# Rows, probabilities, keys and values turned by four 64x64 products instead of one 128x128 transposition, in a hybrid encoder step on one core

## The chip, the cores and the metric

One NeuronCore of a Trainium2 chip runs the whole program in one launch. The metric is the device time of that core in microseconds (us), the median of the runs. All data is float32; the large products are made from two rounded parts (below).

## The reference

One inference step of a one-layer encoder, for 512 prompt tokens and 8 samples of 16 tokens (640 tokens, width 1024). What bears on the change:

```python
h = rmsnorm(x, norm_mix_g);  parts = split_cols(h @ w_in)        # gated delta rule, short convolution, stick-breaking attention
rhs = concatenate([v * beta[..., None], k * (beta * exp(gc))[..., None]])   # delta rule: scaled values and keys
S_new = S * exp(g_last) + einsum('tk,tv->kv', k * exp(g_last - gc)[..., None], v_new)
x = x + concatenate([y_a, y_b, y_c]) @ w_mix_out
h = rmsnorm(x, norm_mem_g); qm = rmsnorm(h @ w_mq, mq_norm_g)    # memory attention, 256 memory tokens, 4 heads
x = x + (softmax(qm @ mem_k.T / sqrt(128)) @ mem_v) @ w_mo
h = rmsnorm(x, norm_ffn_g)
x = x + (silu(dwconv3(h @ w_gate)) * (h @ w_up)) @ w_down
```

## The kernel before

The tokens are five tiles of 128 (four of the prompt, n = 0 to 3, and one of all samples, n = 4, PT in the code). Each engine has an instruction list of its own, written out by hand: TensorE from line 430, ScalarE, GpSimd, and VectorE from line 2136. Engines meet by semaphores: a product bank (PSUM, eight banks of 128x512) is taken with `take`, declared full with `done`, waited for with `filled`, released by its reader and waited for again with `evacuated`. The order on an engine is the program's; nothing is planned at run time.

A large product `a @ w` is three products of rounded parts (hi x hi, hi x lo, lo x hi) in a fast float32 form; ScalarE cuts the hi parts (line 1599 for weights), VectorE the lo parts (line 2150). These products fill most of TensorE's time. Products between plain float32 tiles (in the delta rule and the attentions) each show as two records in the profile.

The places where something is turned from token rows to columns, or back, are:

- **Norm rows**, `turn_rows` (line 571), for norm2 before memory attention and norm3 before the feed-forward part, five tiles each. Eight 128x128 transpositions (line 577) put the 1024 columns of a tile into two banks, four in each. The first bank is declared full after the first four. ScalarE copies each bank to `hhi` (line 1612), VectorE subtracts to get `hlo` and releases it (line 2160). The turns stand between large products: norm2's two first together (lines 1009 and 1010), norm3's between the products with `w_mo` and the first gate products (lines 1171 to 1185).
- **Memory probabilities**, `mem_probs` (line 1088), the same with line 1094, five tiles; ScalarE copies to `probT` (line 2009).
- **Values and keys of the delta rule**, `turn_vk` (line 847), five tiles: four transpositions of the values into bank `Vt`, four of the keys into `Kt` (line 853). VectorE's `vk_part` (line 2420) makes three scaled copies of 128x512: values by beta (2425), keys by bege (2428, after which `kd_ready` lets TensorE's `w_part`, line 885, go on) and keys by kdec (2430).

The order around the delta rule's chunks is: `w_part(4)`, `w_part(0)`, `turn_vk(1)`, then for each chunk i the product `vn` (line 960), `w_part(i + 1)` (line 891), `dS` (971), `o` (977), `turn_vk(i + 2)`.

Products of 64x64 on quarters of the array are in the kernel already: the triangular inverse (`level_products`, line 821) runs them on all four, lines 836 and 842, eight of each line in a step; steps 64-row transpositions (868) and products (875, 881) on one quarter.

```python
                for h in range(HEADS):
                    if y is not None:
                        for g in range(2):
                            last_y = T.matmul(y[half64(1 - g), h, :], lmb[n % LM_RING][half64(g), h, :],
                                              Xb[i][half64(g), h, :], start=True, stop=True)
                    if dx is not None:
                        for g in range(2):
                            last_dx = T.matmul(dx[half64(g), h, :], Xb[i2][half64(g), h, :], XTb[i2][half64(g), h, :],
                                               start=True, stop=True)
```

Of the kernel before, what the change touches and what calls it, by code (L numbers as in the profile page):

```python
# [5 lines left out]
F32 = mybir.dt.float32  # L6
# [5 lines left out]
P = 128  # L12
# [55 lines left out]
def hybrid_step(nc, A, O):  # L68
    ctx = ExitStack()
    with ctx:  # L70
# [208 lines left out]
        def quad(b):  # L279
            return bank[b][:, :].rearrange("p (a b) -> p a b", a=4)  # L280

# [148 lines left out]
        def _(pe):  # L430
# [139 lines left out]

            def turn_rows(kind, n, src, ready):

                pe.wait_ge(s["xn_ready"], ready)
                for g in range(2):
                    b = take((kind, n, g))
                    for j in range(4):
                        ins = T.transpose(bank[b][:, j * P:(j + 1) * P], src[:, (4 * g + j) * P:(4 * g + j + 1) * P],
                                          ident[:, :])
                    done(ins, (kind, n, g))
# [267 lines left out]
            def turn_vk(i):  # L847

                tt = slice(i * P, (i + 1) * P)
                for name, f0 in (("Vt", 8), ("Kt", 4)):  # L850
                    b = take((name, i))
                    for h in range(HEADS):
                        ins = T.transpose(bank[b][:, h * P:(h + 1) * P], qkvz[:, f0 + h, tt], ident[:, :])
                    done(ins, (name, i))
# [54 lines left out]
            def sample_new():  # L909
                pe.wait_ge(s["st_loaded"], 16 * DEC_BATCH)  # L910
                evacuated(pe, ("wT", PT))
                evacuated(pe, ("Vt", PT))
# [26 lines left out]
            def sample_states(h):  # L939
                evacuated(pe, ("Kt", PT))  # L940
# [10 lines left out]
            for i in range(PT):  # L951
                tt = slice(i * P, (i + 1) * P)
                evacuated(pe, ("Vt", i))
# [13 lines left out]
                evacuated(pe, ("Kt", i))  # L967
# [70 lines left out]
            for h, tiles in ((0, (0, 1, 2)), (1, (3, PT))):  # L1038
                for n in tiles:
                    for g in range(2):  # L1040
                        evacuated(pe, ("norm2", n, g))
                across_half(("mq", 0), B_MQ[0], h)
# [45 lines left out]
            def mem_probs(i):  # L1088
                pe.wait_ge(s["prob_ready"], i + 1)
                for g in range(2):  # L1090
                    b = take(("pT", i, g))
# [4 lines left out]
                    done(ins, ("pT", i, g))  # L1096
# [483 lines left out]
        def _(act_e):  # L1580
# [28 lines left out]
            def hi_part(kind, n, dst):  # L1609
                for g in range(2):  # L1610
                    b = filled(e, (kind, n, g))
                    V(dst[:, 4 * g:4 * g + 4], quad(b), ACT.Copy).then_inc(s["h_hi_ready"], 1)
# [303 lines left out]
            for i in range(PT):  # L1916
# [10 lines left out]
                elif i == 2:  # L1927
                    o_part(PT)
                    filled(e, ("Kt", PT - 1))
                    y_hi(0)  # L1930
# [73 lines left out]
            def prob_turned(i):  # L2004
                if i >= 2:
                    filled(e, ("om", i - 2))
                for g in range(2):
                    b = filled(e, ("pT", i, g))
                    V(probT[i % 2][:, 2 * g:2 * g + 2, :, :].rearrange("p h n t -> p (h n t)"), bank[b][:, :], ACT.Copy)\
# [126 lines left out]
        def _(dve):  # L2136
# [18 lines left out]
            def lo_part(kind, n, hi, lo):  # L2155
                for g in range(2):
# [3 lines left out]
                    V.tensor_tensor(lo[:, 4 * g:4 * g + 4], quad(b), hi[:, 4 * g:4 * g + 4].bitcast(F32), ALU.subtract)\  # L2160
# [732 lines left out]
```

## Time and profile before

| | us |
|---|---|
| median of three runs | 947.84 (947.35 to 947.84) |
| the profiled execution | 947.93 |
| its span, first to last instruction | 946.2 |
| TensorE busy | 934.1 (99%) |
| VectorE busy | 648.3 (69%) |
| ScalarE busy | 451.9 (48%) |
| GpSimd busy | 170.1 (18%) |
| transfers | 103.69 MB, 16 engines busy 32% of the span |

The span is shorter than the time of its execution by 1.7 us, which lie before the first and after the last instruction. An engine's busy time is the union of its records. TensorE's records overlap, since one product drains while the next fills, so a record's own duration (some 270 ns for a 128x128 transposition) is not what it costs; the distance from one start to the next is.

### The profile page before, as it was taken

What the parts mean: (1) busy time and instruction counts of PE and PEld (TensorE: products, weight loads), DVE (VectorE), ACT (ScalarE), POOL (GpSimd) and SP (SyncE); (2) the same over time, 40 slices, a digit from 0 to 9 for tenths busy, and PEclk for the clock granted to TensorE, in tenths of its full rate; (3) what the DMA queues carried; (4) which work ended last, traced back from release to release, by engine and by line L of the source; (5) the groups of instructions that cost most, each with busy time, mean ns of one, the idle gap of its engine ahead of it and who ended that gap; (6) DMA issues with size and microseconds to landing.
All of it is one profiled execution on the core that took longest, in us unless ns stands there. A gap on an engine that the chain in (4) does not pass through costs nothing.

```text
span 946.2 us, 16664 instructions
## 1 busy us (share of the span) xinstructions
PE 934.1 (99%) x6807; PEld 847.1 (90%) x6807; DVE 648.3 (69%) x1083; ACT 451.9 (48%) x836; POOL 170.1 (18%) x198
## 2 busy tenths in 40 slices
PE   8999999999999999999999999999999999999998
PEld 7899888998889877899889999999999999888886
DVE  7627888777775556551666999999999999435321
ACT  6634444648565344464655445444444446333310
POOL 0071101103654331000002042222222220000000
PEclk9999999999999999999999999999999999999999
DMA  8624152121104084143903322222222224312221
GB/s 302 225 87 145 56 169 90 48 94 46 45 5 134 2 278 166 61 150 150 317 35 116 132 90 90 89 90 90 76 74 77 87 89 147 152 59 97 76 91 55
DMA packets 73819, 103.69 MB, mean 110 GB/s; under 512 B 2576, under 2 KB 53904, under 8 KB 73360
## 3 DMA queue, kind: packets, MB, share of 16 engines
q1 hardware_dynamic: 73744, 102.63, 32.0%
q8 instruction: 54, 0.88, 0.4%
q14 instruction: 21, 0.17, 0.1%
HBM read 92.27 MB, written 10.35 MB: 108 GB/s over the span
## 4 chain that ended last, share of the span: by engine, by line
PE 90%; DVE 4%; ACT 2%; issue 1%; POOL 1%; DMA 1%; SPq 0%; ACTq 0%; DVEq 0%; POOLq 0%
PE bank L1202 8%; PE bank L1204 8%; PE bank L1203 8%; PE bank L533 7%; PE bank L535 7%; PE bank L534 7%; PE bank L495 6%; PE bank L497 5%; PE bank L496 5%; PE bank L463 3%; PE bank L559 2%; PE bank L561 2%; PE bank L560 2%; PE bank L482 1%; PE bank L481 1%; PE bank L483 1%
## 5 line engine op out<-in xcount | busy, mean ns | idle before, releaser
L2150 DVE TENSOR_TENSOR wlo<-wraw,whi 128x2048 fp32r<-128x2048 f32 (+1 forms) x56 | 126.1, 2253 | 103.1 <-ACT whi L1599 93.8
L1599 ACT ACTIVATE whi<-wraw 128x2048 fp32r<-128x2048 f32 (+1 forms) x58 | 109.3, 1885 | 102.7 <-PE bank L535 72.9
L495 PE MATMUL bank<-hhi,whi 128*128 128x320 f32 x352 | 116.4, 331 | 0.6 <-issue 0.6
L497 PE MATMUL bank<-hhi,wlo 128*128 128x320 f32 x352 | 108.7, 309 | 0.0
L496 PE MATMUL bank<-hlo,whi 128*128 128x320 f32 x352 | 108.7, 309 | 0.0
L495 PEld LDWEIGHTS bank<-hhi,whi 128*128 128x128 f32 x352 | 66.2, 188 | 5.0 <-issue 3.6
L496 PEld LDWEIGHTS bank<-hlo,whi 128*128 128x128 f32 x352 | 66.2, 188 | 3.0 <-issue 2.4
L497 PEld LDWEIGHTS bank<-hhi,wlo 128*128 128x128 f32 x352 | 66.1, 188 | 0.0
L533 PE MATMUL bank<-whi,hhi 128*128 128x512 f32 x150 | 58.4, 389 | 0.0
L534 PE MATMUL bank<-wlo,hhi 128*128 128x512 f32 x150 | 58.4, 389 | 0.0
L535 PE MATMUL bank<-whi,hlo 128*128 128x512 f32 x150 | 58.3, 389 | 0.0
L1567 POOL TENSOR_TENSOR traw_up<-wraw 128x512 f32<-128x512 f32 x10 | 14.3, 1428 | 196.2 <-PE bank L1204 170.7
L1202 PE MATMUL bank<-hhi,whi 128*128 128x320 f32 x152 | 47.1, 310 | 0.0
L1204 PE MATMUL bank<-hhi,wlo 128*128 128x320 f32 x152 | 47.0, 309 | 0.0
L1202 PE MATMUL bank<-shi,whi 128*128 128x320 f32 x152 | 47.0, 309 | 0.0
L1203 PE MATMUL bank<-slo,whi 128*128 128x320 f32 x152 | 47.0, 309 | 0.0
L1204 PE MATMUL bank<-shi,wlo 128*128 128x320 f32 x152 | 47.0, 309 | 0.0
L1203 PE MATMUL bank<-hlo,whi 128*128 128x320 f32 x152 | 47.0, 309 | 0.0
L2524 DVE TENSOR_TENSOR xres<-xres,bank 128x512 f32<-128x512 f32 x30 | 20.1, 685 | 26.4 <-PE bank L535 18.8
L2248 DVE SCALAR_TENSOR_TENSOR act<-cb,flanes,act 128x512 f32<-128x512 f32 x44 | 33.0, 749 | 0.9
L534 PEld LDWEIGHTS bank<-wlo,hhi 128*128 128x128 f32 x150 | 28.2, 188 | 5.9
L533 PEld LDWEIGHTS bank<-whi,hhi 128*128 128x128 f32 x150 | 28.2, 188 | 5.9
(489 smaller groups left out, 2701.9 us busy)
## 6 DMA issues: line engine op xcount, KB each, us to landing
wraw<-in_w_in SPq DMA_DIRECT2D x13, 1024.0 KB, 5.3
wraw<-in_w_gate SPq DMA_DIRECT2D x11, 1024.0 KB, 5.1
wraw<-in_w_up SPq DMA_DIRECT2D x11, 1024.0 KB, 5.1
wraw<-in_w_down SPq DMA_DIRECT2D x10, 1024.0 KB, 5.0
kTs<-in_cache_sb_k SPq DMA_DIRECT2D x8, 512.0 KB, 4.4
vraw<-in_cache_sb_v SPq DMA_DIRECT2D x8, 512.0 KB, 5.0
wraw<-in_w_mix_out SPq DMA_DIRECT2D x4, 1024.0 KB, 6.1
kmT<-in_cache_mem_k SPq DMA_DIRECT2D x8, 512.0 KB, 6.0
```

Source lines behind the costliest of these rows:

```text
L495: T.matmul(o, wh[:, k, cs], hhi[:, k, hs], start=(k == 0), stop=False)
L496: T.matmul(o, wh[:, k, cs], hlo[:, k, hs], start=False, stop=False)
L497: ins = T.matmul(o, wl[:, k, cs], hhi[:, k, hs], start=False, stop=(k == KD - 1))
L533: T.matmul(o, hi[:, t * P:(t + 1) * P], wh[:, kk, :], start=(k == 0), stop=False)
L534: T.matmul(o, hi[:, t * P:(t + 1) * P], wl[:, kk, :], start=False, stop=False)
L535: ins = T.matmul(o, lo[:, t * P:(t + 1) * P], wh[:, kk, :], start=False, stop=(k == nk - 1))
L1202: T.matmul(o, w[0][:, k, :], a[0][:, k, :], start=(k == 0), stop=False)
L1203: T.matmul(o, w[0][:, k, :], a[1][:, k, :], start=False, stop=False)
L1204: ins = T.matmul(o, w[1][:, k, :], a[0][:, k, :], start=False, stop=(k == half_block - 1))
L1599: V(wv(whi, i), wv(wraw, i), ACT.Copy).then_inc(s["w_hi_ready"], 1)
L2150: V.tensor_tensor(wv(wlo, i), wv(wraw, i), wv(whi, i).bitcast(F32), ALU.subtract)\
L2248: V.scalar_tensor_tensor(out=out[:, 0:SEQ], in0=a, scalar=w[:, k:k + 1], in1=out[:, 0:SEQ], op0=ALU.mult, op1=ALU.add)
```

## The change

A new helper turns eight 128x128 pieces, each by four ordinary products with the identity: source rows g (a half of 64), source columns c, to output partitions c, 64 columns wide. Row half g of all eight pieces goes to bank g, so that a bank now holds eight pieces of 64 columns where it held four of 128. Both banks are taken ahead, and both are declared full at the end. Norm rows, memory probabilities of the four prompt tiles, and values with keys use it; the sample tile's probabilities stay as they were. Readers take the new layout with the same number of instructions, except `vk_part`, where each of the three scalings becomes two of half the size, and both banks are released by the last pair.

```diff
+        def eighths(b):
+            return bank[b][:, :].rearrange("p (a b) -> p a b", a=8)
...
+            def turn_quarters(outs, srcs):
+
+                for j, src in enumerate(srcs):
+                    last = []
+                    for g in range(2):
+                        for c in range(2):
+                            ins = T.matmul(bank[use[outs[g]][0]][half64(c), BLOCK * j:BLOCK * j + BLOCK],
+                                           src[half64(g), half64(c)], ident[half64(g), half64(g)], start=True, stop=True)
+                        last.append(ins)
+                for ins, key in zip(last, outs):
+                    done(ins, key)
+
             def turn_rows(kind, n, src, ready):
 
                 pe.wait_ge(s["xn_ready"], ready)
-                for g in range(2):
-                    b = take((kind, n, g))
-                    for j in range(4):
-                        ins = T.transpose(bank[b][:, j * P:(j + 1) * P], src[:, (4 * g + j) * P:(4 * g + j + 1) * P],
-                                          ident[:, :])
-                    done(ins, (kind, n, g))
+                outs = [(kind, n, g) for g in range(2)]
+                for key in outs:
+                    take(key)
+                turn_quarters(outs, [src[:, k * P:(k + 1) * P] for k in range(KD)])
...
             def turn_vk(i):
 
                 tt = slice(i * P, (i + 1) * P)
-                for name, f0 in (("Vt", 8), ("Kt", 4)):
-                    b = take((name, i))
-                    for h in range(HEADS):
-                        ins = T.transpose(bank[b][:, h * P:(h + 1) * P], qkvz[:, f0 + h, tt], ident[:, :])
-                    done(ins, (name, i))
+                outs = [("VKt", i, g) for g in range(2)]
+                for key in outs:
+                    take(key)
+                turn_quarters(outs, [qkvz[:, f0 + h, tt] for f0 in (8, 4) for h in range(HEADS)])
...
-            for h, tiles in ((0, (0, 1, 2)), (1, (3, PT))):
-                for n in tiles:
-                    for g in range(2):
-                        evacuated(pe, ("norm2", n, g))
+            turned = [(n, g) for n in range(NT) for g in range(2)]
+            for h in range(2):
+                for n, g in turned[NT * h:NT * h + NT]:
+                    evacuated(pe, ("norm2", n, g))
                 across_half(("mq", 0), B_MQ[0], h)
...
             def hi_part(kind, n, dst):
                 for g in range(2):
                     b = filled(e, (kind, n, g))
-                    V(dst[:, 4 * g:4 * g + 4], quad(b), ACT.Copy).then_inc(s["h_hi_ready"], 1)
+                    V(dst[:, :, half64(g)], eighths(b), ACT.Copy).then_inc(s["h_hi_ready"], 1)
...
             def vk_part(i):
-                b = filled(dve, ("Vt", i))
                 slots = (smp_v, smp_kb, smp_kd) if i == PT else (scr[i % 2], scr[2 + i % 2], scr[4 + i % 2])
+                bs = [filled(dve, ("VKt", i, g)) for g in range(2)]
                 if 2 <= i < PT:
                     filled(dve, ("dS", i - 2))
-                V.tensor_tensor(slots[0][:, :, :], quad(b), spread(beta[:, i, :], 2, [P, HEADS, P]), ALU.mult)\
-                    .then_inc(bank_free[b], 1)
-                b = filled(dve, ("Kt", i))
-                V.tensor_tensor(slots[1][:, :, :], quad(b), spread(bege[:, i, :], 2, [P, HEADS, P]), ALU.mult)\
-                    .then_inc(s["kd_ready"], 1)
-                V.tensor_tensor(slots[2][:, :, :], quad(b), spread(kdec[:, i, :], 2, [P, HEADS, P]), ALU.mult)\
-                    .then_inc(bank_free[b], 1)
+                for out, heads, scale in ((slots[0], slice(0, 4), beta), (slots[1], slice(4, 8), bege), (slots[2], slice(4, 8), kdec)):
+                    for g, b in enumerate(bs):
+                        ins = V.tensor_tensor(out[:, :, half64(g)], eighths(b)[:, heads, :],
+                                              spread(scale[:, i, :], 2, [P, HEADS, BLOCK]), ALU.mult)
+                        if out is slots[2]:
+                            ins.then_inc(bank_free[b], 1)
+                    if out is slots[1]:
+                        ins.then_inc(s["kd_ready"], 1)
```

What moves in the instruction lists. TensorE at `turn_vk(1)`, before the change (lines 891, 853 and 960 are `w_part`, the turn and `vn`; the number at a bank or buffer tells which one it is):

```order
L891 MATMUL bank5<-XT0_93,scr2_55 128x128 x3
L853 MATMUL bank0<-ident_259,qkvz_191 128x128 [waits bank_free0]
L853 MATMUL bank0<-ident_259,qkvz_191 128x128 x3
L853 MATMUL bank1<-ident_259,qkvz_191 128x128 [waits bank_free1]
L853 MATMUL bank1<-ident_259,qkvz_191 128x128 x3
L960 MATMUL bank2<-scr0_53,XT0_93 128x128 [waits bank_free2,bank_free5,bank_free7]
L960 MATMUL bank2<-scr0_53,XT0_93 128x128 x3
L891 MATMUL bank3<-XT1_94,scr3_56 128x128 [waits bank_free3,kd_ready,bank_free2]
```

The same place in the changed kernel, where lines 907 and 976 are `w_part` and `vn`:

```order
L907 MATMUL bank5<-XT0_93,scr2_55 128x128 x3
L580 MATMUL bank0<-ident_259,qkvz_191 64x64 [waits bank_free1,bank_free0]
L580 MATMUL bank0<-ident_259,qkvz_191 64x64
L580 MATMUL bank1<-ident_259,qkvz_191 64x64 x2
L580 MATMUL bank0<-ident_259,qkvz_191 64x64 x2
...
L976 MATMUL bank2<-scr0_53,XT0_93 128x128 [waits bank_free5,bank_free2,bank_free7]
L976 MATMUL bank2<-scr0_53,XT0_93 128x128 x3
L907 MATMUL bank3<-XT1_94,scr3_56 128x128 [waits bank_free3,kd_ready,bank_free2]
```

Eight instructions became thirty-two, two to a bank in turn, and the neighbours stand where they stood. VectorE's scalings for the same turn, before:

```order
L2462 TENSOR_TENSOR sqG1_160<-yb_195 128x640
L2425 TENSOR_TENSOR scr1_54<-bank0,beta_297 128x512
L2428 TENSOR_TENSOR scr3_56<-bank1,bege_306 128x512
L2430 TENSOR_TENSOR scr5_58<-bank1,kdec_305 128x512
L2492 COPY stP0_131<-bank4 128x512
```

and in the changed kernel:

```order
L2485 TENSOR_TENSOR sqG1_160<-yb_195 128x640
L2449 TENSOR_TENSOR scr1_54<-bank0,beta_297 128x4x64
L2449 TENSOR_TENSOR scr1_54<-bank1,beta_297 128x4x64
L2449 TENSOR_TENSOR scr3_56<-bank0,bege_306 128x4x64
L2449 TENSOR_TENSOR scr3_56<-bank1,bege_306 128x4x64
L2449 TENSOR_TENSOR scr5_58<-bank0,kdec_305 128x4x64
L2449 TENSOR_TENSOR scr5_58<-bank1,kdec_305 128x4x64
L2515 COPY stP0_131<-bank4 128x512
```

The first of them needs both banks now, and `kd_ready` comes behind four instructions instead of two.

## Rows read from the trace of the kernel before

**Rows 1.** The page: the chain that ended last, by engine.
```profile
PE 90%; DVE 4%; ACT 2%; issue 1%; POOL 1%; DMA 1%; SPq 0%; ACTq 0%; DVEq 0%; POOLq 0%
```

**Rows 2.** Span and mean granted TensorE clock.
```profile
core 0: 946.2 us, clock 1.000
```

**Rows 3.** Groups by line and form, TensorE: count | busy us, mean ns | idle before.
```profile
L836 PE MATMUL bank<-Xb,lmb 64*64 64x64 f32 x368 | 14.0, 222 | 0.4 <-issue 0.4
L577 PE MATMUL bank<-ident,xn 128*128 128x128 f32 x80 | 10.3, 273 | 0.0
```

**Rows 4.** Timeline, TensorE, turn of norm3's last tile: start us, us, records.
```profile
521.22 0.31 PE L483 MATMUL bank<-hhi,wlo 128*128 128x320 f32 x1
521.36 1.04 PE L577 MATMUL bank<-ident,xn 128*128 128x128 f32 x8
522.15 0.39 PE L481 MATMUL bank<-hhi,whi 128*128 128x320 f32 x1
522.38 0.31 PE L482 MATMUL bank<-hlo,whi 128*128 128x320 f32 x1
```

**Rows 5.** Timeline, TensorE, 32 quarter products of the triangular inverse.
```profile
261.50 0.31 PE L496 MATMUL bank<-hlo,whi 128*128 128x320 f32 x1
261.64 0.31 PE L497 MATMUL bank<-hhi,wlo 128*128 128x320 f32 x1
261.88 0.27 PE L836 MATMUL bank<-Xb,lmb 64*64 64x64 f32 x2
...
262.05 0.23 PE L836 MATMUL bank<-Xb,lmb 64*64 64x64 f32 x2
...
262.75 0.23 PE L836 MATMUL bank<-Xb,lmb 64*64 64x64 f32 x2
...
262.97 0.42 PE L495 MATMUL bank<-hhi,whi 128*128 128x320 f32 x1
263.23 0.31 PE L496 MATMUL bank<-hlo,whi 128*128 128x320 f32 x1
```

**Rows 6.** Timeline, TensorE, turns of the delta rule among plain float32 products.
```profile
287.98 1.08 PE L868 MATMUL bank<-ident,XT 64*64 64x64 f32 x16
288.99 1.09 PE L853 MATMUL bank<-ident,qkvz 128*128 128x128 f32 x8
290.01 1.90 PE L875 MATMUL bank<-Xb,LT 64*64 64x64 f32 x29
...
296.23 1.04 PE L853 MATMUL bank<-ident,qkvz 128*128 128x128 f32 x8
...
298.26 1.13 PE L891 MATMUL bank<-XT,scr 128*128 128x128 f32 x8
...
300.37 1.06 PE L977 MATMUL bank<-qkD,scr 128*128 128x128 f32 x8
301.26 1.04 PE L853 MATMUL bank<-ident,qkvz 128*128 128x128 f32 x8
302.13 1.24 PE L898 MATMUL bank<-sqG,same 128*128 128x320 f32 x4
```

**Rows 7.** Timeline, VectorE, scalings of one turn, and two smaller operations from a bank.
```profile
283.56 0.85 DVE L2448 TENSOR_TENSOR XT<-XTb,bank 64x256 f32<-64x256 f32 x2 [0.38 <-PE bank L842]
...
296.87 0.69 DVE L2425 TENSOR_TENSOR scr<-bank,beta 128x512 f32<-128x512 f32 x1 [1.02 <-PE bank L853]
297.48 0.68 DVE L2428 TENSOR_TENSOR scr<-bank,bege 128x512 f32<-128x512 f32 x1
```

**Rows 8.** Timeline, TensorE, three waits after turns: idle us and releaser in brackets.
```profile
401.14 0.47 PE L1022 MATMUL bank<-whi,mhi 128*128 128x512 f32 x1 [0.89 <-DVE wlo L2150]
...
475.74 0.47 PE L559 MATMUL bank<-whi,omhi 128*128 128x512 f32 x1 [0.32 <-DVE wlo L2150]
...
481.95 0.47 PE L559 MATMUL bank<-whi,omhi 128*128 128x512 f32 x1 [0.58 <-DVE omlo L2598]
```

**Rows 9.** The same timeline, the last turn of probabilities before that third wait.
```profile
480.33 1.04 PE L1094 MATMUL bank<-ident,probs 128*128 128x128 f32 x8
```

More of the change, by code:

```diff
@@ L849, in turn_vk, with values_keys_done @@
                 tt = slice(i * P, (i + 1) * P)
-                for name, f0 in (("Vt", 8), ("Kt", 4)):
-                    b = take((name, i))
-                    for h in range(HEADS):
-                        ins = T.transpose(bank[b][:, h * P:(h + 1) * P], qkvz[:, f0 + h, tt], ident[:, :])
-                    done(ins, (name, i))
+                outs = [("VKt", i, g) for g in range(2)]
+                for key in outs:
+                    take(key)
+                turn_quarters(outs, [qkvz[:, f0 + h, tt] for f0 in (8, 4) for h in range(HEADS)])
+            def values_keys_done(i):
+                for g in range(2):
+                    evacuated(pe, ("VKt", i, g))
             for n in range(len(LM_ORDER) + LAG):
@@ L911, in sample_new @@
                 evacuated(pe, ("wT", PT))
-                evacuated(pe, ("Vt", PT))
+                values_keys_done(PT)
                 b = take(("vn", PT), long=True)
@@ L939, in sample_states @@
             def sample_states(h):
-                evacuated(pe, ("Kt", PT))
+                values_keys_done(PT)
                 pe.wait_ge(s["vm_ready"], h + 1)
@@ L952, in _ @@
                 tt = slice(i * P, (i + 1) * P)
-                evacuated(pe, ("Vt", i))
+                values_keys_done(i)
                 evacuated(pe, ("wT", i))
@@ L966, in _ @@
                 evacuated(pe, ("vn", i))
-                evacuated(pe, ("Kt", i))
+                values_keys_done(i)
                 vn = scr[8 + i % 2]
@@ L1089, in mem_probs @@
                 pe.wait_ge(s["prob_ready"], i + 1)
+                outs = [("pT", i, g) for g in range(2)]
+                if i < PT:
+                    for key in outs:
+                        take(key)
+                    turn_quarters(outs, [probs[i % 2][:, h, nb * P:(nb + 1) * P] for h in range(HEADS) for nb in range(2)])
+                    return
                 for g in range(2):
-                    b = take(("pT", i, g))
+                    b = take(outs[g])
                     for j in range(4):
@@ L1095, in mem_probs @@
                                           ident[:, :])
-                    done(ins, ("pT", i, g))
+                    done(ins, outs[g])
             def mem_values(i):
@@ L1928, in _ @@
                     o_part(PT)
-                    filled(e, ("Kt", PT - 1))
+                    filled(e, ("VKt", PT - 1, 1))
                     y_hi(0)
@@ L2008, in prob_turned @@
                     b = filled(e, ("pT", i, g))
-                    V(probT[i % 2][:, 2 * g:2 * g + 2, :, :].rearrange("p h n t -> p (h n t)"), bank[b][:, :], ACT.Copy)\
+                    V(probT[i % 2][:, :, :, half64(g)].rearrange("p h n t -> p (h n) t"), eighths(b), ACT.Copy)\
                         .then_inc(bank_free[b], 1)
@@ L2159, in lo_part @@
                     b, _ = use[(kind, n, g)]
-                    V.tensor_tensor(lo[:, 4 * g:4 * g + 4], quad(b), hi[:, 4 * g:4 * g + 4].bitcast(F32), ALU.subtract)\
+                    V.tensor_tensor(lo[:, :, half64(g)], eighths(b), hi[:, :, half64(g)].bitcast(F32), ALU.subtract)\
                         .then_inc(bank_free[b], 1)
```

## The prediction

> **What bounds the kernel now.** I read the page first. TensorE is busy for 934.1 of 946.2 us, and 90% of the chain that ended last is its own work [rows 1]. So the kernel is a queue of products, and a change pays only as far as it makes TensorE's list shorter, or removes one of the few waits in it. The granted clock is 1.000 over the span, the higher level of 2.4 GHz [rows 2]; there is no slow stretch to win back. The second thing to read is what a turn costs as a distance between starts, since durations overlap (a mean of 273 ns for a transposition whose 80 records make 10.3 us busy) [rows 3]. The third is where TensorE waits near a turn, for there a longer or shorter turn is free [rows 8]. The changed stretches lie between 283 and 530 us; the 416 us of feed-forward work behind them only shift.
>
> **What eight transpositions cost.** Between large products, norm3's last turn starts at 521.36 and the gate product behind it at 522.15 [rows 4]. From the start of the last large product ahead (521.22) to the second one behind (522.38) it is 1.16 us, of which two starts of such products, some 0.145 us each (261.50 to 261.64 [rows 5], 521.22 to 521.36), would have been there anyway: 0.87 us, or 0.109 each. Among plain float32 products it is the same 0.87 us, 301.26 to 302.13 [rows 6].
>
> **What thirty-two quarter products cost.** The triangular inverse holds the very burst: 16 calls of line 836 and 16 of line 842 on all four quarters, between the same large products. From 261.64 to 263.23 it is 1.59 us [rows 5], less the same 0.29: 1.29 us. Two things are in it. First the stream: twelve steps from 262.05 to 262.75, so 58 ns for a group of four records, one on each quarter. A product leaves two records (368 for 184 calls) [rows 3], a transposition one (80 for 80). So a piece needs two groups, 117 ns, where one transposition took 109: eight pieces are 0.93 us against 0.87, **0.06 us more**. The four quarters do run at once, but the plain product goes twice through them. Second the change of width: 1.29 less 0.93 is **0.36 us** for going in and out. It is seen as 0.24 us ahead of the first quarter product where 0.145 is the step, and 0.26 from 262.97 to 263.23 behind them [rows 5]. A turn among large products thus costs 0.42 us more.
>
> Among plain float32 products the two changes cost less. Eight transpositions between quarter work take 1.02 us (288.99 to 290.01) against 0.87, and the sixteen one-quarter transpositions ahead, 56 ns apart, 1.01 us against 0.90 [rows 6]. Half a change each way, with the slower first step behind: I take 0.29 us for both, so 0.35 us more for such a turn. Bounds for a turn: 0.06 if the width changes cost nothing, 0.42 if they always cost what they do at large products.
>
> **The sum, place by place** (TensorE, in order).
>
> - *Norm2.* Tiles 0 and 1 form one burst: 2 x 0.06 + 0.36 = 0.48. Tile 2: 0.42. Tile 3 is followed by an idle 0.89 us until 401.14, for a weight cut on VectorE [rows 8] that comes from ScalarE's cut, which waited for an earlier product: 0.42 hides there, 0. Tile 4, between memory-key products: 0.42. Together 1.3.
> - *Norm3.* Tile 0 already follows a change of width (32-wide products) and has transpositions behind: one way only, 0.2. Tiles 1 to 4: 4 x 0.42 = 1.7. Together 1.9.
> - *Probabilities.* Four turns, 0.35 + 0.2 (products of 32 columns follow, a change that is there already) + 0.42 + 0.42 = 1.4 of TensorE's time. But VectorE and ScalarE pace this stretch: TensorE waits 0.32 and 0.58 us idle at 475.74 and 481.95 [rows 8]. By the distance of starts the second is 0.75 (480.33 plus 0.87 is 481.20 [rows 9]), so an idle time leaves out some 0.17, and the two are 1.2 in all. What comes out is 0.2.
> - *Values and keys.* Turn 4 follows quarter work, so loses one change it paid (0.15) and gains the dear one behind (0.22) with 0.06: 0.1. Turn 0 stands between quarter products: it loses both changes, 0.06 - 0.29 = -0.2. Turns 2 and 3 are among plain products: 0.35 each. Turn 1 is longer by a wait: `w_part(1)` at 298.26 starts 0.1 us after VectorE's second scaling ends (297.48 + 0.68) [rows 6, 7]. That scaling chain started 0.64 us into the turn (296.87), with the first bank. Now both banks come at the end, about 1.25 us into it (0.09 + 0.05 + 0.93 and the drain), 297.5. Then four half scalings stand before `kd_ready` instead of two. A half costs between 0.30 us (half of the 0.61 between two starts) and 0.43 (two 64x256 operations from a bank in 0.85) [rows 7]; I take 0.40, nearer to the row of that size. 297.5 + 1.6 + 0.1 = 299.2, 0.95 later; the product behind waits a little for a copy of ScalarE's that is there by then, so I take 0.8. Bounds 0.4 and 1.0. Together 1.4. The other scalings have idle VectorE around them (1.02 us before this one [rows 7]); without it they would cost 0.6 a turn.
> - *Readers.* ScalarE and VectorE keep their counts at norm rows and probabilities, but start some 0.6 us later, since the first bank no longer comes early. The waits of TensorE behind a turn are those of rows 8, and none names these readers, since other products stand between; so 0. The finer wait for norm2 (2.5 tiles instead of 3 for the first query half) frees nothing: other products cover it. No transfer moves.
>
> Sum: 1.3 + 1.9 + 0.2 + 1.4 = **4.8 us more**. The profiled execution took 947.93, 0.09 above the median of the runs shown, so 952.7, or **952.6** as a median. A measurement of this kernel tells 0.2% (1.9 us) from no change: below 945.9 is faster, above 949.7 slower.
>
> **The rivals.**
>
> - *One group does a piece* (the other side). A product with the identity, whose records may pair differently from those of the inverse, goes through the four quarters once, 58 ns for a piece. A tile then costs 0.47 us. With the changes of width kept, a single turn at large products is 0.83 against 0.87 (six of them -0.2), the double saves 0.4, norm3's first turn 0.3 and values and keys 1.0, and the sum is -1.9: 946.0, no change. If these changes also fade, it saves 0.40 on each of the some 14 tiles that nothing else paces, 942. It decides from a piece below 64 ns on, where the 0.36 are earned back. For it: nothing but that the moving side is always the same. Against: two records for every plain product in the trace. Chance 0.11, of which 0.08 for the faster form. The Trainium skill, page "TensorEngine Tiling (Array Packing)", section "Theoretical Speedup", gives a factor of up to 2 for each side of 64 or less, so 4 for these; as an estimate, eight pieces in 0.22 us, which lands in the same rival.
> - *Cover is larger than I see.* The readers' and the later stages' waits take most of it, or the changes of width are half of what the inverse shows, since its bursts start with waits for banks: 0.15 to 0.2 a turn, some 1.5 us in all. 949.3, no change. For it: the first step after each wait is slow anyway. Against: the exit, 0.26 for 0.147, has no wait. Chance 0.1.
> - *A new wait.* Late banks push ScalarE and VectorE where they pace TensorE (481.95) and around each chunk; a further 0.6 us at five places, 955.6. For it: the second bank's copy ends 0.6 later everywhere. Against: idle readers before most turns. Chance 0.1.
> - *Quarters in one row half do not overlap.* The inverse never issues two neighbours of one row half; here all do. Pairs in turn would double the stream: 0.93 more for 19 tiles, 968. Against: in the inverse all four still run within one group. Chance 0.04. The Trainium skill, page "TensorE: Matmul & The Clock Gate", section "Terms", has transpose mode four times faster than a plain product for float32, which speaks against this change and lands here too: a piece would take four groups, not two, an estimate. The rows have two records per product; the sum goes by them.
> - That the change does not do what it says is excluded: the lists show the 32 products and six scalings.
>
> **How the numbers follow.** The forecast has 0.65, its own range 951 to 954.5 (0.06 to 0.42 a turn would be wider, but the burst of the same size fixes it). Faster: 0.08, the first rival's faster form. Same: 0.03 of its weaker form and 0.1 of the second, 0.13. Slower: 0.65 + 0.1 + 0.04 = 0.79. The range, 949.0 to 956.0, takes in the new wait and the upper half of the second rival, and leaves out 946.0, 942, 968 and the lower half, 0.2 in all.
>
> **What would show it.** Right: the product line of the new helper with 1216 records (19 tiles x 64), groups of four 58 ns apart; 1.29 us between large products; 64x64 at 0.24 ahead and 0.25 behind; `w_part(1)` about 0.95 us later against its turn's start; the idle of 0.89 before the first memory-key product nearly halved; the wait before 481.95 gone or small; a half scaling near 0.40 us. Wrong: 608 records, or groups of 29 ns; a turn under 0.9 us; idle growing behind turns; or a gain in the feed-forward part, which the change does not touch.

## The result and the profile after

The changed kernel takes **955.37 us** (median of four runs, 955.09 to 956.57), the kernel before 947.84 (947.35 to 948.23) beside it: a ratio of 1.0081, interval 1.0066 to 1.0096. That is 7.5 us more; the forecast was 4.8 more, 952.6, with a range to 956.0, and the forecast's own part of it ended at 954.5. Of all executions of all variants one stands apart (row halves, 1295 us at a mean granted clock of 0.663), and the ratios leave it out. The profiled execution took 955.46 with a span of 953.7. The page of the changed kernel, its parts 1, 3 (queues) and 4 (chain):

```profile
PE 941.1 (99%) x7871; PEld 851.5 (89%) x7871; DVE 649.5 (68%) x1098; ACT 451.9 (47%) x836; POOL 170.1 (18%) x198
...
q8 instruction: 62, 1.02, 0.5%
...
PE 92%; DVE 3%; ACT 2%; POOL 1%; issue 1%; DMA 1%; SPq 0%; ACTq 0%; POOLq 0%; DVEq 0%
```

TensorE is still the chain [rows 1]; it has 7.0 us more of busy time (934.1 before) and 1064 records more (6807 before). The second row is the one I had not thought about: the page calls queue 8 "instruction", and it moved 62 packets of 16 KB where the kernel before moved 54:

```profile
q8 instruction: 54, 0.88, 0.4%
```

These packets are TensorE's own list. Its weight loads, products and semaphore operations together are 16051 records, 62.7 times 256; before they were 13910, 54.3 times 256. In all fourteen traces the packets are this quotient to within one. The span's mean granted clock is 1.000, as in [rows 2].

The new helper's line, and one turn between large products (start, us, records), which answers to [rows 4]:

```profile
L580 PE MATMUL bank<-ident,xn x640: 218/218/267, 389.5 to 529.5; 64*64 64x64 f32 x160
L580 PE MATMUL bank<-ident,qkvz x320: 218/218/268, 283.7 to 316.0; 64*64 64x64 f32 x160
L580 PE MATMUL bank<-ident,probs x256: 218/218/267, 465.9 to 487.4; 64*64 64x64 f32 x128
```

```profile
528.32 0.31 PE L486 MATMUL bank<-hhi,wlo 128*128 128x320 f32 x1
528.56 1.16 PE L580 MATMUL bank<-ident,xn 64*64 64x64 f32 x64
529.65 0.42 PE L484 MATMUL bank<-hhi,whi 128*128 128x320 f32 x1
529.90 0.31 PE L485 MATMUL bank<-hlo,whi 128*128 128x320 f32 x1
```

640 + 320 + 256 are the 1216 records forecast, two for each product. The turn goes in after 0.24, streams for 0.94 (16 groups 58 ns apart), and out in 0.15 + 0.25: 528.32 to 529.90 is 1.58, less two steps 1.29. That is the figure taken from the inverse.

The turn that costs most is the delta rule's second, with the wait behind it. It answers to [rows 6], where `w_part(1)` starts 2.03 us after its turn (296.23 to 298.26). TensorE's products, its weight loads and VectorE's scalings:

```profile
297.35 1.16 PE L580 MATMUL bank<-ident,qkvz 64*64 64x64 f32 x64
298.44 1.16 PE L976 MATMUL bank<-scr,XT 128*128 128x128 f32 x8
301.53 1.05 PE L907 MATMUL bank<-XT,scr 128*128 128x128 f32 x8 [1.93 <-issue]
```

```profile
298.88 0.53 PEld L976 LDWEIGHTS bank<-scr,XT 128*128 128x128 f32 x4
300.16 0.19 PEld L907 LDWEIGHTS bank<-XT,scr 128*128 128x128 f32 x1 [0.76 <-issue]
301.53 0.86 PEld L907 LDWEIGHTS bank<-XT,scr 128*128 128x128 f32 x7 [1.19 <-issue]
```

```profile
298.67 0.76 DVE L2449 TENSOR_TENSOR scr<-bank,beta 128x256 f32<-128x256 f32 x2 [1.96 <-PE bank L580]
299.34 0.75 DVE L2449 TENSOR_TENSOR scr<-bank,bege 128x256 f32<-128x256 f32 x2
300.01 0.75 DVE L2449 TENSOR_TENSOR scr<-bank,kdec 128x256 f32<-128x256 f32 x2
```

Here it is 4.18 us after its turn. The semaphore wait ended at 300.16, when the first weights of `w_part(1)` were loaded, just behind the keys' second half scaling (299.34 + 0.75). That is the forecast wait. But the second load comes only at 301.53. Nothing in the profile holds it ("issue"), and its data is there: the first load had the same wait in front.

### The profile page after: what moved, and what is told of

It reads as the page before. It is cut to its first block, busy times and chain, and to the rows that moved or that the text cites. A ratio compares the mean times of both kernels' runs of the same rounds, so it can differ in the third digit from the quotient of the medians.

```text
span 953.7 us, 18825 instructions
## 1 busy us (share of the span) xinstructions
PE 941.1 (99%) x7871; PEld 851.5 (89%) x7871; DVE 649.5 (68%) x1098; ACT 451.9 (47%) x836; POOL 170.1 (18%) x198
## 4 chain that ended last, share of the span: by engine, by line
PE 92%; DVE 3%; ACT 2%; POOL 1%; issue 1%; DMA 1%; SPq 0%; ACTq 0%; POOLq 0%; DVEq 0%
PE bank L1224 8%; PE bank L1226 8%; PE bank L1225 8%; PE bank L536 7%; PE bank L538 7%; PE bank L537 7%; PE bank L498 6%; PE bank L500 5%; PE bank L499 5%; PE bank L466 3%; PE bank L580 2%; PE bank L562 2%; PE bank L564 2%; PE bank L563 2%; PE bank L484 2%; PE bank L485 1%
```

## The experiments

Two theories of the missing 2.7 us. **W**, the waits of late banks and half scalings are longer than I had them, at `w_part(1)` above all. **F**, instruction fetch: the list is brought in pieces of 256 records, and a list with 128 records a turn where 16 stood runs dry. F came from counting TensorE's records in order of start. Every gap of TensorE that nothing else explains lies ahead of a record that is 193 to 195 modulo 256 (short: record 195; a count by start is off by one or two), 1.2 to 1.6 us behind the landing of a packet of queue 8. The reverse holds too: in none of the fourteen traces does TensorE pass this place sooner than 1.2 us behind the landing of the packet that belongs to it (record 256k + 449 and packet k, both counted from 0). The first four experiments set F against W, the later ones settle one point each.

**Norm rows alone** (values, keys and probabilities as before; the edit for values and keys, against the changed kernel):

```diff
-                outs = [("VKt", i, g) for g in range(2)]
-                for key in outs:
-                    take(key)
-                turn_quarters(outs, [qkvz[:, f0 + h, tt] for f0 in (8, 4) for h in range(HEADS)])
+                for name, f0 in (("Vt", 8), ("Kt", 4)):
+                    b = take((name, i))
+                    for h in range(HEADS):
+                        ins = T.transpose(bank[b][:, h * P:(h + 1) * P], qkvz[:, f0 + h, tt], ident[:, :])
+                    done(ins, (name, i))
...
```

> The norm rows alone are turned by quarter products; probabilities, values and keys as before. Both theories price these ten tiles alike, from the trace of the changed kernel: 0.54 + 0.43 + 0 + 0.39 us in norm2 and 0.17 + 0.45 + 0.40 + 0.49 + 0.39 in norm3, so 3.3 us over the kernel before, 951.1, ratio 1.0034. If the stretches cost less alone (late banks in one place pushing another), under 2.5 us.

950.91 (five runs), ratio 1.0033 (1.0020 to 1.0046): 3.0 us more, my sum for the ten turns being 3.2. This part of the forecast stands.

**Values and keys alone** (norm rows and probabilities as before):

> Values and keys alone are turned by quarter products, with the halved scalings. Theory W (width changes, a longer stream and scalings that start late, as forecast): 1.4 us over before, 949.2. Theory F (besides, TensorE's sequencer waits for its next piece of instruction list, 16 KB for 256 instructions, since a turn now holds 128 instructions instead of 16): the instruction list up to w_part(1) is that of the changed kernel, so the gap in issue of some 1.4 us between its first and second weight load returns, and the whole is 2.5 to 3.3 us over before, 950.3 to 951.1.

951.59, ratio 1.0034 (1.0021 to 1.0047): 3.7 more, against 1.4 in my sum, and above F's 950.3 to 951.1 too. TensorE's timeline at `w_part(1)`, here line 909:

```profile
297.24 1.16 PE L580 MATMUL bank<-ident,qkvz 64*64 64x64 f32 x64
298.33 1.16 PE L978 MATMUL bank<-scr,XT 128*128 128x128 f32 x8
301.97 1.05 PE L909 MATMUL bank<-XT,scr 128*128 128x128 f32 x8 [2.48 <-issue]
```

The wait is longer than in the change (2.48 for 1.93) with the same scalings. W has no reason for that. The packet of queue 8 starts at 299.43 here and at 298.93 in the change.

**The list shifted.** 32 idle quarter products near the program's start, 128 records, and nothing else:

```diff
                 T.matmul(bank[7][:, 0:P], ones[:, :], ones[:, :], start=True, stop=True)
+            for n in range(8):
+                for g in range(2):
+                    for c in range(2):
+                        T.matmul(bank[7 - g][half64(c), 0:BLOCK], ones[half64(g), half64(c)], ones[half64(g), 0:BLOCK],
+                                 start=True, stop=True)
```

> The changed kernel with 32 idle quarter products on a constant added to TensorE's list at its very start, where TensorE waits for data anyway: 128 instructions, half of a 16 KB piece. Theory F: the gap in w_part(1) moves elsewhere or changes its size by 0.5 us or more, other gaps in issue between 255 and 300 us move too, and total time changes by up to 1.5 us either way. Theory W: the gap stays where it is with its 1.4 us within 0.2, since the semaphores are the same; total within 0.5 us of the changed kernel.

952.11, ratio 1.0042 (1.0028 to 1.0056): with more work, 3.3 us faster than the change. W allowed 0.5; F has the direction open and had named up to 1.5, so its size was missed as well. `w_part(1)`, here line 912, has no gap behind its first load:

```profile
296.52 1.16 PE L580 MATMUL bank<-ident,qkvz 64*64 64x64 f32 x64
297.61 1.16 PE L981 MATMUL bank<-scr,XT 128*128 128x128 f32 x8
299.37 1.13 PE L912 MATMUL bank<-XT,scr 128*128 128x128 f32 x8 [0.59 <-issue]
```

It starts 2.85 us after its turn, 0.82 later than in the kernel before. So W is real there and as large as the forecast had it (0.8), and the other 1.3 of 4.18 were the list.

**Keys scaled first**, so that `kd_ready` needs two half scalings fewer:

```diff
-                for out, heads, scale in ((slots[0], slice(0, 4), beta), (slots[1], slice(4, 8), bege), (slots[2], slice(4, 8), kdec)):
+                for out, heads, scale in ((slots[1], slice(4, 8), bege), (slots[0], slice(0, 4), beta), (slots[2], slice(4, 8), kdec)):
```

> The changed kernel with VectorE's two scalings of the keys by bege ahead of those of the values, so that kd_ready comes 0.66 us earlier. Theory W (w_part(1) waits for the scaling): w_part(1) starts 0.66 us earlier and the time falls by 0.5 to 0.7 us. Theory F (the instructions arrive later than the scaling): its first weight load starts 0.66 us earlier, the second not, and the time stays within 0.2 us.

955.24, ratio 1.0075 (1.0060 to 1.0090): no gain measured. In its profiled execution `w_part(1)` does start sooner, 2.48 us after its turn, but TensorE ran at the lower clock level in the stretch before (granted clock 0.50 from 294.8 to 296.7), which cost 1.5 us there. The packet landed at 298.96, 1.9 us before TensorE reached its records, so the list held nothing up at this place. All four runs have a mean clock of 0.998 or 0.999, against two of four in the change. The run tells little of W's size.

**One weight load held back** behind `w_part(1)`:

```diff
                 D(stS[:, bt, :, :], A["state_gdn"][bt].rearrange("h k v -> k h v")).then_inc(s["st_loaded"], 16)
+            filled(sp, ("wT", 1))
             load_w(B_OUT[1][0])
```

> The changed kernel, where SyncE holds back one load, the 1 MB of w_mix_out behind the eight state loads, until the product w_part(1) is done. TensorE's list is the same instruction for instruction. Fetch theory: the piece of TensorE's list that w_part(1) needs waits behind data on the DMA engines (there the fetch began 6.4 us after the last gap, elsewhere 1.3 to 1.9); with the states' 2 MB done by about 295 it begins near 296 instead of 298.93, the gap of 1.37 us ahead of w_part(1)'s second weight load goes, and the time falls by about 1.4 us, to 954.0. Rival (the gap is TensorE's own, from the place in its list or from the late scalings): the gap stays at 1.3 to 1.4 us, the fetch may come earlier, and the time is that of the changed kernel, 955.4. Second rival (the fetch begins at a fixed distance ahead of need and not behind data): fetch and gap stay as they are.

954.20, ratio 1.0066 (1.0054 to 1.0079): 1.2 less than the change, as F had it (1.4), though the two intervals overlap. Among runs with a mean clock of 1.000 it is about 2 less (953.0 and 953.5 here, 955.1 and 955.5 in the change). In the trace the packet starts at 297.08 and not 298.93, and `w_part(1)`'s second load follows its first without a gap. This execution had the lower clock level too (0.50 at 296.7 to 298.4), so the place can't be compared in time.

**Row halves.** The same pieces turned by two transpositions on half the rows:

```diff
                     for g in range(2):
-                        for c in range(2):
-                            ins = T.matmul(bank[use[outs[g]][0]][half64(c), BLOCK * j:BLOCK * j + BLOCK],
-                                           src[half64(g), half64(c)], ident[half64(g), half64(g)], start=True, stop=True)
+                        ins = T.transpose(bank[use[outs[g]][0]][:, BLOCK * j:BLOCK * j + BLOCK],
+                                          src[half64(g), :], ident[half64(g), half64(g)])
```

> The changed kernel, where each piece is turned by two transpositions on the two row halves of the array (64 rows in, 128x64 out) instead of four quarter products: 16 instructions a tile of one record each instead of 32 of two. All else (banks, eighths, half scalings) as in the change. If the two halves run at once, as the four quarters did, a step of 64 columns is 56 ns for a pair and a tile streams in 0.45 us instead of 0.93, so with the 0.36 of going in and out a turn is 0.81 at large products (0.87 in the kernel before). That gives against the changed kernel 0.48 a tile, some 16 tiles unpaced, 7.5 us, and with the lists' pieces elsewhere (1 us either way) 947 to 949: the loss gone, and what is left is the late banks. If the halves do not overlap, a tile takes 0.90 and the time is 953 to 955.

947.73 (median of eleven runs), ratio 0.9997 (0.9987 to 1.0006): all the loss is gone. The turn that answers to [rows 4]:

```profile
521.36 0.31 PE L486 MATMUL bank<-hhi,wlo 128*128 128x320 f32 x1
521.60 0.72 PE L579 MATMUL bank<-ident,xn 64*128 64x64 f32 x16
522.25 0.42 PE L484 MATMUL bank<-hhi,whi 128*128 128x320 f32 x1
522.50 0.31 PE L485 MATMUL bank<-hlo,whi 128*128 128x320 f32 x1
```

A pair takes 62 to 65 ns and a tile streams in 0.49 to 0.52 us: both halves run at once, and each transposition leaves one record, 16 for a tile where the quarter products leave 64. With the same change of width, 521.36 to 522.50 is 1.14, less two steps 0.85; the whole transpositions took 0.87. The stream halves and the change of width takes it back.

**The kernel before with the shifted list:**

> The kernel before, with the same 32 idle quarter products near the start that took 3.2 us off the changed kernel (64 instructions more in TensorE's list, nothing else). The kernel before shows three gaps of TensorE of its own between 264 and 277 us (0.43, 0.66, 0.43), each at a record that is 195 modulo 256, 1.3 to 1.6 us behind the landing of a piece of the list. Fetch theory: the three gaps move to other places; there they may be covered or not, so the time changes by up to 1.4 us either way, with every new gap again at 195 modulo 256, and 947 to 948.5 is likeliest. Rival (gaps belong to these products, not to the place in the list): they stay at the same products and the time is unchanged at 947.9 (plus 0 to 0.5 for the added work).

947.23 (eleven runs), ratio 0.9994 (0.9985 to 1.0002). The three gaps of 0.43 to 0.66 us are gone and two of 0.36 and 0.30 are there, at 269.30 and 273.69, again at record 195. What it saves, 0.7, can't be told from nothing. (The idle products are 128 records, not the 64 I gave there.)

**Row half by row half**, the order of the 32 products changed so that only two quarters can work at once:

```diff
-                for j, src in enumerate(srcs):
-                    last = []
-                    for g in range(2):
+                for g in range(2):
+                    for j, src in enumerate(srcs):
                         for c in range(2):
...
-                for ins, key in zip(last, outs):
-                    done(ins, key)
+                    done(ins, outs[g])
```

> The changed kernel with the same 32 quarter products of a turn in another order: first the 16 of the upper rows (two quarters, side by side in columns), then the 16 of the lower rows, and the first bank reported full halfway. It measures whether all four quarters work at once. If they do in the change, this order halves it: a group of two quarters takes 58 ns as a group of four did, a tile streams in 1.87 instead of 0.93 us, and 0.93 for 16 unpaced tiles make 970, less some 0.3 a turn where readers waited for the first bank. If the order of issue does not matter (the engine reorders, or the rate is one of issue, 14.5 ns a record), the time is 955 or less.

966.32, ratio 1.0196 (1.0182 to 1.0210). A turn, here between 512-wide products:

```profile
524.10 1.91 PE L579 MATMUL bank<-ident,xn 64*64 64x64 f32 x64
525.94 0.50 PE L562 MATMUL bank<-whi,omhi 128*128 128x512 f32 x1
```

1.84 us from the turn's start to the next product, where four quarters take 1.09. So in the change all four do work at once, and the rival of quarters that do not overlap is out. (The time expected was 970 less some 0.3 a turn.)

**Norm rows and probabilities by quarters**, values and keys as before:

> The changed kernel with norm rows and probabilities by quarter products, but values and keys as in the kernel before. The part with norm rows alone took 950.9; this adds the probabilities. The trace of the changed kernel has 0.57 us between the first of their turns and the last, 0.4 of it a gap at a place in the instruction list, which is elsewhere here. Forecast 951.2; by my sum 951.1; if VectorE's and ScalarE's later banks cost what the third rival of the prediction said (0.6 a chunk), 952.5 and more.

951.28, ratio 1.0039 (1.0026 to 1.0053). The probabilities cost 0.4 over norm rows alone, near the 0.2 of the sum.

**The list shifted by half as much** (`range(4)` for `range(8)`, 64 records):

> The changed kernel with half as many idle quarter products near the start, 16, so that every later place of TensorE's list moves by 64 records and not by 128. (The 32 of the earlier run were 128 records, loads and products counted: 16179 against 16051.) Fetch theory: the gaps go where a record is 195 modulo 256 now, the one of w_part(1) into the middle of the values' and keys' second turn (297.8), where everything behind it (the banks, the scalings, w_part(1)) is late too. If the fetch there again comes 6 us after the last one's gap, the time is 956 to 958, above the changed kernel with its smaller list; if it comes after 1.6 to 2.2 us as in the run shifted by 128, no gap is left and the time is 952 to 953. In neither case is there a gap of over 0.5 us at w_part(1)'s second load. Rival (the gap belongs to w_part(1), whatever its place in the list): 1.4 us there again and 955.4.

955.06, ratio 1.0078 (1.0066 to 1.0091): neither number of F's, and close to its rival's 955.4. But the trace is against the rival: `w_part(1)` starts 2.85 us after its turn (296.70 to 299.55), without a gap. The time is lost in a place that no expectation had named, between memory scores of the samples:

```profile
470.63 2.55 PE L1149 MATMUL bank<-kmT,qz 128*32 128x256 f32 x43
474.75 0.83 PE L1149 MATMUL bank<-kmT,qz 128*32 128x256 f32 x9 [1.58 <-issue]
```

The last weight load ahead of the gap starts 2.17 us earlier, and the gap ends at record 9410, which is 194 modulo 256. The kernel shifted by 128 has 0.40 there. F's rule for where a gap can be holds; how long the gap is depends on when the piece is fetched. The windows of queue 8 show that the packet starts after 472, 4.15 us after the record 195 of the piece before (467.88), with the DMA engines full. The queues in two windows, and the busy times of one (its last two columns are the DMA engines' share and GB/s):

```profile
q1 hardware_dynamic: 718, 1.38, 100.7%
```

```profile
q1 hardware_dynamic: 225, 0.43, 92.2%
q8 instruction: 1, 0.02, 6.0%
```

```profile
464.00:472.00 8.00, 8.00 (x193) 6.71 (x196) 5.28 (x15) 4.62 (x13) 0.31 (x1) 1.00 0.99 344
```

The first row is the whole of 467.9 to 472, without a packet of queue 8, the next two are 472 to 473.3.

The same trace shows a second wait, which is W's. Behind turn 0 the products of line 902 wait for a bank that VectorE's last scalings release:

```profile
289.88 2.03 PE L896 MATMUL bank<-Xb,LT 64*64 64x64 f32 x32
292.11 2.04 PE L902 MATMUL bank<-XT,Xb 64*64 64x64 f32 x32 [0.21 <-DVE scr L2454]
```

```profile
291.70 0.27 PE L881 MATMUL bank<-XT,Xb 64*64 64x64 f32 x1
```

Here they start 2.23 us after line 896; in the kernel before (second fence, its line 881) they start 1.69 us after line 875 at 290.01 [rows 6]. The run shifted by 128 has 2.23 as well and the change 2.24, so this 0.5 us is there wherever the list's pieces fall.

**Quiet load queues** there, with the same list:

```diff
                 load_mem_k(bt)
+            filled(sp, ("ms", PT, 1))
             for bt in range(3, 7):
                 load_mem_v(bt)
             for t in range(2):
                 evacuated(sp, ("mv", 0, t))
             D(O["p_mem_v"].rearrange("(t p) c -> p t c", p=P), memv[:, :, :]).then_inc(s["out_mv"], 16)
             load_w(B_GU[0][0])
-            filled(sp, ("ms", PT, 1))
```

> The kernel of e11_shifted_by_64, where SyncE holds back four loads of memory values, the output of memory values and the load of w_gate (3.5 MB in all, which run from 463 to 475) until the samples' memory scores are done at some 475.5. TensorE's list is the same instruction for instruction. It settles what delays a piece of the list. In e11_shifted_by_64 the record 9155 (195 modulo 256) starts at 467.88, the next piece is fetched only 4.15 us later, at 472.03, and TensorE stands 2.17 us ahead of record 9410 until 474.75. If a fetch waits behind the data of the load queue (DMA engines 0.97 to 1.00 busy there), it now begins within 1.1 to 2.1 us of 467.9, as in the stretch 260 to 285 without traffic, lands before 471, the gap of 2.17 goes and the time falls by about 2 us, to 953.1 (less if the late loads are waited for). If it always begins some 4 us behind in this part of the list, whatever the queues carry, gap and time stay, 955.1.

953.14, ratio 1.0053 (1.0040 to 1.0067): 1.9 us less than the same list with busy queues, the number expected. Queue 8 from 467.9 to 469.8, TensorE from 464 to 473.3, and its timeline:

```profile
q8 instruction: 1, 0.02, 3.2%
```

```profile
464.00:472.00 8.00, 8.00 (x187) 1.00 0.28 102
472.00:473.30 1.30, 1.30 (x26) 1.00 0.00 0
```

```profile
469.69 3.42 PE L1149 MATMUL bank<-kmT,qz 128*32 128x256 f32 x60
473.04 2.05 PE L1134 MATMUL bank<-probT,memv 128*128 128x128 f32 x16
```

The packet starts 1.05 us behind record 195 (467.37), lands before 470, and the gap is gone. Against the kernel before beside each run (947.69 and 948.20) the saving is 2.4. F is shown, and at this place also that the piece of TensorE's list came late because of the data of the loads.

**A version that beats both:** row halves for norm rows and probabilities, whole transpositions for values and keys, and the idle products.

> The attempt at a version that beats both. Norm rows and probabilities turned by two transpositions on the row halves, as in e6_row_halves; values and keys, their scalings and their two banks as in the kernel before; and the 32 idle quarter products near the start. From the rows of e6_row_halves beside those of the kernel before, a turn between large products is 0.03 us shorter than eight whole transpositions (1.30 against 1.33, and 1.14 against 1.17), the double one of norm2 0.41 shorter (1.81 against 2.22), norm3's first 0.1: some 0.8 us in all. The idle products gave the kernel before 0.7. Together 1.5: 946.4, a ratio of 0.9984. Rival: the readers, which start later because both banks fill at the end, take it back at the probabilities, and only the 0.7 of the idle products stays: 947.2.

946.61 (eleven runs), ratio 0.9990 (0.9981 to 0.9998): faster than the kernel before by 1.1 us, of 1.5 expected. Only the double turn gains much: from the large product ahead to the second behind it (384.48 to 386.29) it is 1.81 us.

```profile
384.48 0.39 PE L564 MATMUL bank<-whi,mxlo 128*128 128x512 f32 x1
384.80 1.22 PE L579 MATMUL bank<-ident,xn 64*128 64x64 f32 x32
385.95 0.50 PE L562 MATMUL bank<-whi,mxhi 128*128 128x512 f32 x1
386.29 0.40 PE L563 MATMUL bank<-wlo,mxhi 128*128 128x512 f32 x1
```

The kernel before takes 2.22 for the same. The gain is small, close to what this measurement tells from nothing, and 0.7 of it is what the idle products alone did for the kernel before.

## Why the prediction was right, and where it was short

The time came 2.7 us above the sum, outside the forecast's own 951 to 954.5. It fell inside the range only because the range had room for the rival of a new wait at 955.6: the direction is the forecast's merit, that 955.4 lies in the range is luck.

**Direction, stream and change of width: right.** Two records a product, 58 ns a group, 0.36 us in and out at large products, 1.29 for a turn: all as read from the inverse's burst. Compared place by place in the two traces, norm2 lost 1.36 us (1.3 forecast), norm3 1.90 (1.9), the probabilities 0.57 (0.2), of which a gap of the list's is 0.4. Values and keys lost 3.3 (1.4), and 0.4 came ahead of the first turn: 0.7 in gaps of the inverse, less 0.3 by which this execution started sooner. Of the waits of [rows 8] the two at the probabilities are gone, as said. The wait of 0.89 became 0.67, a quarter less and not half, though that turn cost nothing, as forecast. A half scaling takes 0.33 us (0.67 between the starts of two pairs), not the 0.40 taken.

```profile
405.78 0.47 PE L1038 MATMUL bank<-whi,mhi 128*128 128x512 f32 x1 [0.67 <-DVE wlo L2172]
```

**The step that failed is the term for values and keys**, "Turn 1 is longer by a wait ... so I take 0.8. Bounds 0.4 and 1.0", and with it "together 1.4". The wait at `w_part(1)` itself was right: it starts 0.82 later against its turn in the shifted kernels, where the forecast had 0.95 and took 0.8. The turn lost 2.15 in the change (4.18 for 2.03), and values and keys 3.3 in all. Two things were left out of the sum. The smaller is the wait behind turn 0, 0.5 us, which "The other scalings have idle VectorE around them" ruled out: both banks are released only by the last pair of scalings. With it values and keys lose 2.1 between the two kernels with 32 idle products, where the list holds up neither. The larger, 1.3 us at `w_part(1)`, is what a longer list costs by its length: a turn has 128 records where it had 16, half a piece of the list. In the inverse and the turns behind it TensorE passes a piece in some 4 us, and the fetch of the next needs some 4 from record 195 (start 1.1 to 2.1 later, 0.9 to 1.5 to land, 1.2 to 1.6 until it runs); behind full load queues it took 8.9 at `w_part(1)` and 6.8 at 477.93. So behind the inverse the list runs dry at 292.55 (which costs nothing, being inside the wait behind turn 0), at 301.53 and at 477.93. The trace of before showed three such gaps, at 264.64, 268.43 and 276.80, in the inverse, and the page had the row of queue 8. I read neither.

**The size from the other side.** Both kernels with the idle products, where few gaps are left, differ by 952.11 - 947.23 = 4.9 us, beside the forecast's 4.8. The change lost another 3.3 to its list's place, the kernel before 0.7, and 4.9 + 3.3 - 0.7 is the 7.5 measured. That 4.9 meets 4.8 so closely is partly luck: the term for values and keys was 0.7 short even there.

**The rivals.** One group a piece: out, the 1216 records. Quarters that do not overlap: out by the order of row halves, which costs 10.9 us more. The Trainium skill, page "TensorE: Matmul & The Clock Gate", section "Terms", has transpose mode four times faster for float32; here a piece by plain products on quarters takes 117 ns, by transpositions on row halves 65, and by one whole transposition 109. No pair of these is apart by four: plain products and transpositions on parts of the array differ by 1.8, and on the whole array by 2.0 (four plain 128x128 products take 0.89 us, 300.37 to 301.26 in [rows 6], 0.22 each). A larger cover: out. A new wait behind late banks gave the nearest number (955.6), but mostly not by its mechanism: of its five waits one came, the 0.5 us behind turn 0, while norm rows and probabilities cost what the sum said.

**What stays open.** Two packets of the run shifted by 128 started 1.6 and 2.2 us behind record 195 although the DMA engines were full (290.76, 298.86), and one of the kernel before 0.4 us behind it (426.22), so full queues do not always delay them by 4. By what order they are served is not shown. That holding back the weight load saved 1.2 to 2 us is measured, but how much of it is the list is not, since the one trace of that run has the lower clock at the place.

## What to carry to other kernels

Before splitting an operation into many small ones, count the instructions: four records for each plain float32 product (two loads, two products). Where an engine passes 256 records in less than some 4 us, or while large loads fill the queues, its list can run dry, and a change elsewhere in the program moves the place. A kernel that is to be compared to 0.3% should be timed with its list shifted once. Narrow tiles pay by the burst: going in and out cost 0.36 us, so join turns before splitting them. If a turn has to be split, use transpositions on row halves: 16 records a tile where quarter products have 64.

## What the runs showed of the hardware

- TensorE's list comes in packets of 16384 bytes on queue 8, one for 256 records. TensorE's unexplained gaps (0.30 to 2.17 us) all lie at record 193 to 195 modulo 256, 1.2 to 1.6 us behind a landing.
- Where 256 records last long, the packet mostly starts ahead of record 195. In the inverse (259 to 282 us, load queues empty) it starts 0.4 to 2.2 us behind record 195, elsewhere with empty load queues at most 3.4. With load queues full it starts up to 7.2 behind, in 92 such cases 2.5 in the median. Holding back 3.5 MB of loads took 1.9 us off a kernel whose TensorE did not wait for any of them there.
- Two row halves run transpositions at once, 62 to 65 ns for two of 64 rows and 128 columns; one alone of 128x128 takes 109.
- In three of the variants the profiled execution fell to the lower clock level (1.2 GHz) for some 3.5 us near 295, behind an idle 0.60 us that the others have too; `w_part(4)` and `w_part(0)` took 3.5 us instead of 2.0. The stretches of the row-half variant (the last three columns: granted clock, DMA share, GB/s):

```profile
290.00:293.00 3.00, 2.62 (x42) 1.00 0.99 273
293.00:294.80 1.80, 1.54 (x7) 0.52 1.19 308
294.80:296.70 1.90, 1.90 (x11) 0.56 1.13 324
```

The idle share ahead does not tell them apart. Of 290 to 293 TensorE was busy for 2.62, 2.80 and 2.86 us in the three that fell, and for 2.67 to 3.00 in those that kept the higher level. Why one falls is open.
